# Channel mixers: in the loop chunks the up projection keeps a weight block stationary and streams 256 tokens

## The reference

```
def swiglu(x, w_in, w_out):
    gate, up = jnp.split(x @ w_in, 2, axis=-1)
    return (jax.nn.silu(gate) * up) @ w_out
...
    for l in range(DEPTH):
        x = layer_norm(ALPHA * x + 0.5 * swiglu(x, ffn1_w_in[l], ffn1_w_out[l]), ...)
        y = diff_pool_mixer(...) if l % 2 == 0 else hgrn2_mixer(...)
        x = layer_norm(ALPHA * x + y, ...)
        x = layer_norm(ALPHA * x + 0.5 * swiglu(x, ffn2_w_in[l], ffn2_w_out[l]), ...)
```

## Time and profile before

| | us |
|---|---|
| median of 3 runs (lowest, highest) | 1044.91 (1044.62, 1045.3) |
| span of the profiled execution | 1041.9 |
| TensorE matmul busy | 1007.7 (97%) |
| TensorE weight loads busy | 832.8 (80%) |
| VectorE busy | 651.4 (63%) |
| ScalarE busy | 495.9 (48%) |

### The profile page before, as it was taken

How to read it: one execution, slowest core, us unless ns; L and a number is a source line. 1 busy time by engine, 2 the same in 40 slices (tenths; PEclk the granted TensorE clock), 3 DMA queues, 4 the chain that set the end, 5 groups by cost and what they waited for, 6 DMA issues and landing times.

```text
span 1041.9 us, 12880 instructions
## 1 busy us (share of the span) xinstructions
PE 1007.7 (97%) x4748; PEld 832.8 (80%) x4748; DVE 651.4 (63%) x823; ACT 495.9 (48%) x548; POOL 44.3 (4%) x73
## 2 busy tenths in 40 slices
PE   5999999999999999999999999999999799999996
PEld 4888888887788888887888888788888678888885
DVE  4565455886767545567955446887977776454455
ACT  4455544346447544442543434387677424434430
POOL 2000000100210000001000000100000110000000
PEclk9999999999999999999999999999999999999999
DMA  9765556453655655563575565453423436656521
GB/s 312 263 206 196 187 176 202 162 202 117 206 203 191 222 191 191 181 231 123 179 233 195 188 193 194 138 169 107 141 93 111 139 117 224 196 173 201 177 104 40
DMA packets 132820, 184.29 MB, mean 177 GB/s; under 512 B 5808, under 2 KB 112448, under 8 KB 132656
## 3 DMA queue, kind: packets, MB, share of 16 engines
q1 hardware_dynamic: 129872, 173.56, 50.4%
q0 software_dynamic: 2624, 9.66, 2.7%
q10 hardware_dynamic: 288, 0.59, 0.2%
HBM read 182.73 MB, written 1.05 MB: 176 GB/s over the span
## 4 chain that ended last, share of the span: by engine, by line
PE 86%; DVE 7%; ACT 3%; DMA 2%; issue 1%; POOL 1%; SPq 0%; DVEq 0%; ACTq 0%
PE psum L1188 27%; PE psum L1190 26%; PE psum L1189 26%; DVE w_lo L658 2%; PE psum L1254 2%; PE psum L1536 2%; ACT w_hi L366 1%; DMA raw<-in_ffn_w_in 1%; DVE stats L677 1%; PE psum L1183 1%; DVE x_tok L675 1%; PE psum L1523 1%; PE psum L1524 1%; DMA raw<-in_c_w_in 1%; ACT L548 0%
## 5 line engine op out<-in xcount | busy, mean ns | idle before, releaser
L658 DVE TENSOR_TENSOR w_lo<-raw,w_hi 128x2048 fp32r<-128x2048 f32 x164 | 374.9, 2291 | 182.6 <-ACT w_hi L366 182.2
L1188 PE MATMUL psum<-w_hi,xT_hi 128*128 128x512 f32 x960 | 383.3, 399 | 7.0 <-DVE xT_lo L665 5.3
L1189 PE MATMUL psum<-w_lo,xT_hi 128*128 128x512 f32 x960 | 375.3, 391 | 0.0
L1190 PE MATMUL psum<-w_hi,xT_lo 128*128 128x512 f32 x960 | 375.2, 391 | 0.0
L366 ACT CAST w_hi<-raw 128x2048 fp32r<-128x2048 f32 x164 | 311.8, 1908 | 14.5 <-DMA raw<-in_ffn_w_in 10.1
L1188 PEld LDWEIGHTS psum<-w_hi,xT_hi 128*128 128x128 f32 x960 | 181.0, 189 | 46.7 <-DVE xT_lo L665 7.7
L1190 PEld LDWEIGHTS psum<-w_hi,xT_lo 128*128 128x128 f32 x960 | 180.9, 188 | 39.3
L1189 PEld LDWEIGHTS psum<-w_lo,xT_hi 128*128 128x128 f32 x960 | 181.2, 189 | 35.3
L376 ACT ACTIVATE ffn_tok<-psum 128x256 f32<-128x256 f32 x88 | 33.8, 384 | 243.2 <-PE psum L1190 243.1
L1188 PE MATMUL psum<-w_hi,hT_hi 128*128 128x512 f32 x352 | 138.3, 393 | 0.0
L1190 PE MATMUL psum<-w_hi,hT_lo 128*128 128x512 f32 x352 | 137.2, 390 | 0.0
(11 more groups left out here) (159 smaller groups left out, 590.2 us busy)
## 6 DMA issues: line engine op xcount, KB each, us to landing
raw<-in_ffn_w_in SPq DMA_DIRECT2D x176, 512.0 KB, 4.7
raw<-in_ffn_w_out SPq DMA_DIRECT2D x88, 512.0 KB, 4.1
raw<-in_c_w_in SPq DMA_DIRECT2D x32, 512.0 KB, 4.8
raw<-in_ab_w_in SPq DMA_DIRECT2D x16, 512.0 KB, 4.8
raw<-in_ab_w_o SPq DMA_DIRECT2D x8, 512.0 KB, 3.7
raw<-in_c_w_o SPq DMA_DIRECT2D x8, 512.0 KB, 3.8
ln_gb<-in_ln_gain POOLq DMA_DIRECT2D x6, 512.0 KB, 4.7
ln_gb<-in_ln_bias POOLq DMA_DIRECT2D x6, 512.0 KB, 5.8
```

The lines of the kernel that those rows point to most:

```text
L658: nc.vector.tensor_tensor(w_lo[:, n % RING], raw[:, n % RAW], w_hi[:, n % RING].bitcast(F32), ALU.subtract).then_inc(lo_ready, 1)
L1188: nc.tensor.matmul(dst, a_hi, b_hi, start=first, stop=False)
L1189: nc.tensor.matmul(dst, a_hi, b_lo, start=False, stop=False)
L1190: return nc.tensor.matmul(dst, a_lo, b_hi, start=False, stop=last)
```

## The change

In the loop chunks, `project` is replaced by `project_T`: a 128x128 block of weights (`w_hi`/`w_lo`) is stationary and the activations of all 256 tokens move. It runs for two feature blocks j = 0 and 1 in place of two token tiles, and for each of the eight blocks k it makes the gate block and the up block (g = 0 and 1), each with three passes. The tile `G[j]` then has features on partitions and holds gate and up of 256 tokens. SiLU and the product are written as before, so `ffn_tok[:, 1]` now holds the hidden tile feature-major. `hidden_T` is gone from the loop; ScalarE and VectorE make `hT_hi` and `hT_lo` straight from `ffn_tok` (named `hid_T`). VectorE waits for its own last `hidT_lo` before it writes the hidden tile again. Chunks 0, 1 and 10 and all else are as before; the counts of `hidT_done` follow.

```
+N_HIDDEN_T = 4
+        hid_T = ffn_tok[:, 1].rearrange("p j f -> p (j f)")
...
             def ffn_hidT(name, c, par):
-                act.wait_ge(hidT_done, c + (SILUS[name] * NH + 1))
+                act.wait_ge(hidT_done, c + (SILUS[name] * N_HIDDEN_T + 1))
                 nc.scalar.copy(hT_hi[:, par], T[0]).then_inc(hidT_hi, 1)
+
+            def ffn_hid_hi(name, c, par):
+
+                act.wait_ge(hid_ready, c * 2 + (2 * SILUS[name] * NC + 2))
+                nc.scalar.copy(hT_hi[:, par], hid_T).then_inc(hidT_hi, 1)
...
                         split_hi(n + 2, i)
-                        ffn_hidT(name, c, par)
+                        ffn_hid_hi(name, c, par)
...
                         for t in range(TT):
                             split_lo(n + t, i)
+                            dve.wait_ge(hidT_lo, c + SILUS[name] * NH)
                             ffn_hidden(name, t, G[t], c * 2 + t, ffn_tok[:, 1, t])
                         split_lo(n + 2, i)
-                        ffn_hidT(name, c, par)
+                        ffn_hidT(name, c, par, hid_T)
...
+            def project_T(n, i, j):
+
+                for kh in range(2):
+                    pe.wait_ge(lo_ready, i * RING + (n + kh + 1))
+                    slot = (n + kh) % RING
+                    for k in range(4):
+                        kk = 4 * kh + k
+                        for g in range(2):
+                            cs = slice(k * 512 + g * FC + j * P, k * 512 + g * FC + (j + 1) * P)
+                            ins = three_passes(G[j][:, g * SEQ:(g + 1) * SEQ], w_hi[:, slot, cs], w_lo[:, slot, cs],
+                                               xT_hi[:, kk], xT_lo[:, kk], kk == 0 and g == 0,
+                                               kk == KB - 1 and g == 1)
+                    if kh == 1:
+                        ins.then_inc(chunk_done[j], 1)
+                    elif j == 1:
+                        ins.then_inc(unit_used, 1)
...
-                        for t in range(TT):
-                            pe.wait_ge(hid_ready, c * 2 + (hid - 1 + t))
-                            project(n, i, t, G[t])
+                        for j in range(2):
+                            pe.wait_ge(hid_ready, c * 2 + (hid - 1 + j))
+                            project_T(n, i, j)
                         for t in range(TT):
                             down(name, n + 2, i, c - 1, (1 + par) % 2, t, False, False)
-                        hidden_T(name, ((c * 2, ffn_tok[:, 1, 0]), (c * 2 + 1, ffn_tok[:, 1, 1])))
```

More of the change, by code:

```diff
@@ L427, in ffn @@
                         split_hi(n + 2)
-                    act.wait_ge(hidT_done, c + t + (SILUS[name] * NH + 1))
+                    act.wait_ge(hidT_done, 2 + t + (SILUS[name] * N_HIDDEN_T + 1))
                     nc.scalar.copy(tile_half(hT_hi[:, 0], t), tile_half(T[0], t)).then_inc(hidT_hi, 1)
@@ L710, in ffn_hidden, with ffn_hidT @@
                 nc.vector.tensor_tensor(hid, g[:, FC:2 * FC], ffn_tok[:, 0, t], ALU.mult).then_inc(hid_ready, 1)
-            def ffn_hidT(name, c, par):
+            def ffn_hidT(name, c, par, hid=T[0]):
                 dve.wait_ge(hidT_hi, c + (SILUS[name] * NH + 1))
-                nc.vector.tensor_tensor(hT_lo[:, par], T[0], hT_hi[:, par].bitcast(F32),
+                nc.vector.tensor_tensor(hT_lo[:, par], hid, hT_hi[:, par].bitcast(F32),
                                         ALU.subtract).then_inc(hidT_lo, 1)
```

## The result

The changed kernel takes 1048.38 us (median of 7, 1046.93 to 1048.97), the kernel before 1044.91 us (7 runs in the same comparison): ratio 1.0036, 95% interval 1.0027 to 1.0045. It is slower by 3.5 us (2.8 to 4.7 by the interval). The direction is the one forecast; the size is less than half of the 8.1 us forecast.

A forecast was written before the change was run, and what follows sets the result against it. TensorE's instruction stream bounds the loop chunks; 5.44 + 96 x 0.121 = 17.06 us a chunk against 16.81, +0.25 x 32 = +8.0 us on 1044.9, so 1053 us, range 1028 to 1068.

The forecast's parts named there:

- The bound: Loop chunks are bound by TensorE's instruction stream: 16.81 us of unbroken TensorE work a chunk.
- Removed, 0.49 us a chunk: Loop chunks lose four transposes and what follows them, 0.49 us a chunk, with nothing in their place on TensorE.
- Other engines: Casts and remainders in the loop lie beside TensorE; without that cover they would be some 1.3 us a chunk.
- p: Distance between starts of the loop's 256-column projection matmuls, 96 a chunk, taken as 0.121 us.
- fixed cost of each pair: Each weight load and matmul in the loop pays 0.0134 us beyond its columns, giving 0.1201 us at 256 columns.
- The allowance: 0.001 us added to the distance of the loop's short matmuls for less even spacing near short matmuls.
- break-even: Start distance of 256-column matmuls at which the new loop chunk equals the old 16.81 us: 0.1184 us.
- The span and the median: Whole kernel: median of the runs stays 3.0 us above the profiled span, which becomes 1049.9 us.
- Rival A: Loop's 256-column matmuls start 0.112 to 0.1134 us apart, surcharge shrinking with columns: 1025 to 1029 us; chance 0.26.
- Rival D: No difference: loads in the loop pair up so that p lies within 0.7 ns of 0.1184; chance 0.07.
- Rival B: Load and matmul in the loop's projection hinder each other, p 0.127 us, +26 us: 1071 us; chance 0.12.
- Rival C: Each of 12 backward branches of the loops waits for an instruction fetch, 36 us more: 1089 us; chance 0.05.

The follow-up runs named there:

- the split and alternating versions: Kernel before, projection matmuls split into 384 and 128 columns: 1135.29 us; changed kernel, high and low activations moving together, long and short matmuls in turn: 1043.86 us.
- without transposes: Changed kernel with the old projection (tokens stationary, 512 weight columns moving) put back in the loop, transposes still gone: 1026.97 us, ratio 0.9825.
- the split one: Kernel before, transposes kept, each 512-column matmul of the loop's projection split into two of 256 columns: 1063.26 us, ratio 1.017.

## Why the prediction was right in direction and wrong in size

*The bound* was read rightly: TensorE is busy for the whole of each loop stretch before and after, and nothing else entered.

*Removed, 0.49 us a chunk:* right, measured 0.49 by itself.

*Other engines:* right in that they cost nothing. The short matmuls have no idle time before them, and in a chunk of 16.98 us VectorE is busy for 8.08 and ScalarE for 7.41. The casts, 622 ns for `hT_hi` and 684 for `hT_lo`, are longer than the 477 and 573 forecast; beside TensorE's stream that has no effect.

*p, the failed step.* The prediction derived 0.1201 us from a fixed cost of each pair and then wrote: "I take p = 0.121: the fixed cost, with 0.001 for the less even spacing near short matmuls". The allowance has no ground in this loop: in 96 equal matmuls the spacing is even, 0.1199. The uneven spacing of phase C that it was taken from stands in a row of mixed lengths; no run varied that row, but the split and alternating versions show uneven starts of the same kind where lengths change. With 3.07 us for each nanosecond, the allowance and the rounding above it are 3.4 us of the forecast 8.0. With 0.1199 the prediction's own sum is 5.44 + 11.51 = 16.95 us a chunk, +4.5 us. The measured chunk has 0.03 us more, since the first down matmuls after the short ones start further apart, and the loops as a whole gave +4.9. Near the break-even of 0.1184 an allowance of one part in a hundred adds three quarters to the answer.

*The span and the median.* The remaining 1.5 us lie between the spans' +5.0 and the medians' +3.5. The prediction took the 3.0 us between the span before and the median as a fixed distance. Every profiled execution whose own time is on record took only 1.8 or 1.9 us more than its span (1048.69 and 1046.9 for the changed kernel, 1028.69 and 1026.9 without transposes, 1066.21 and 1064.4 for the split one). By that the execution before was one of about 1043.7 us, 1.2 below its median, while that of the changed kernel lay 0.3 above. What the typical execution before does in these 1.2 us no trace shows.

*Rival A* (a surcharge that shrinks with columns) is out: p is 0.1199, and 384 columns stand at 0.1733. The fixed size of the charge holds for 128 stationary columns and 256 to 512 moving ones. But the reading of it as a cost of the pair as such, or as a thing of fp32r, was wrong, as the table above shows; the number was right, its cause stays open. To that extent the direction was luck: with 64 stationary columns the same fixed cost would have been forecast, and 0.1133 lies on the other side of the break-even. *Rival D* (0.1184 within 0.7 ns) is out by 0.8 ns.

The section "Back-to-back issue gap" (page "TensorE: Matmul & The Clock Gate" of the Trainium skill) gives its formula for an isolated matmul; by it the change would have gained some 29 us. The pairs of load and matmul here do not follow it: bf16 stood at 0.1133 and fp32r at 0.1200 where it gives 0.109. The section "Weight-path perf modes" of the same page of the Trainium skill says that a fast weight load is used for 128 columns of a type other than fp32. The loads in the table agree: bf16 takes 97 ns for 128 columns and 108 for 64.

*Rival B* (load and matmul hinder each other, 0.127) is out by p. *Rival C* (fetching at the backward branch) is out: 26 packets for the longer program, 3 more than before and not one for each of 12 branches, and no gap in the loop. The window of two blocks that the section "Instruction fetch mechanics" (page "Runtime: NRT & Kernel Launch" of the Trainium skill) describes does not show in this kernel; whether a loop body of 480 matmul and load instructions leaves it, no row here tells.

## What to carry to other kernels

A reshaping that keeps the columns and doubles the matmuls is decided by what one pair of weight load and matmul costs beyond its columns: count the pairs, and multiply by a distance read from long, even trains of the same type and the same stationary width, entered in the same way. Where the answer lies near break-even, take the number as it is read, without an allowance, and give the range both signs. If operands must be split in high and low parts, let both parts move in one matmul and group matmuls of equal length; here that turned +0.36% into -0.64%. Compare chunks of the timeline when a step is smaller than the spread of executions.

## What was not expected of the hardware

- Distances between starts depend on the pattern. Even fp32r trains with 128 stationary columns lock at 0.2267, 0.1733 and 0.1200 us for 512, 384 and 256 columns. After a change of length, the next eight long ones average 0.230.
- They also depend on what came before the train. Long and short ones in turn take 0.3467 us for two in the first loop chunk of each mixer, after transposes, and 0.3533 in the 28 others, after a down projection. With 32 stationary columns it is 0.1133 and 0.1179 us in the same places.
- Shorter loads are not steadily better: 64 stationary columns stand at 0.1133 us in all chunks, 32 columns never below it, under the same 256 moving ones.
- Loading 64 bf16 columns takes longer (108 ns) than loading 128 (97 ns).
